# Forty-eight projections a layer placed between the steps of an attention, and its head norm taken with tokens on partitions

## The reference

```python
h = rmsnorm(x, norm_g)
aq, ak, av, az, bqk, bv, bi, bf, bo, bz, ga, gb = split(h @ w_in)      # 1024 -> 10256
# branch a: 8 heads, two score maps of 64 each, values of 128
q, k = rope(rmsnorm(aq)), rope(rmsnorm(ak))
a = softmax(causal(q1 k1')) - lam * softmax(causal(q2 k2'))
oa = rmsnorm(a @ av, attn_norm_g) * (1 - lam_init) * silu(az)
# branch b: mLSTM of 8 heads, in its quadratic form
mq, mk = split(silu(causal_conv(bqk, conv_w, conv_b)))                 # 4 taps
hb = (mq mk' * exp(gates)) @ bv / max(|row sum|, exp(-m))
hb = sigmoid(bo) * rmsnorm(hb, mlstm_norm_g) * silu(bz)
u = sigmoid(ga) * (oa @ w_out_a) + sigmoid(gb) * (hb @ w_out_b)
x = x + u @ w_o
```

## Time and profile before

| | |
|---|---|
| median of three runs | 2130.93 us |
| profiled execution, span | 2131.4 us |
| PE busy | 2042.5 us (96%) |
| DVE, ACT, POOL busy | 1151.3, 909.2, 291.2 us |
| the two attentions of the second block | 110.3 and 110.8 us, to the last scores' transposes |

### The profile page before, as it was taken

How to read it: one execution, slowest core, us unless ns; L and a number is a source line. 1 busy time by engine, 2 the same in 40 slices (tenths; PEclk the granted TensorE clock), 3 DMA queues, 4 the chain that set the end, 5 groups by cost and what they waited for, 6 DMA issues and landing times.

```text
span 2131.4 us, 28672 instructions
## 1 busy us (share of the span) xinstructions
PE 2042.5 (96%) x11112; PEld 1557.0 (73%) x11112; DVE 1151.3 (54%) x2057; ACT 909.2 (43%) x1685; POOL 291.2 (14%) x354
## 2 busy tenths in 40 slices
PE   7999999899999998999999899999999899999998
PEld 2443334378888885546899899995599899975798
DVE  3327442287777532462555575665545677555544
ACT  2235331151423324452555565544453565545442
POOL 1015000000000000230000042202213052002303
PEclk9999999989999999999999999995599999975799
DMA  8320232234554431201454443540044334520141
GB/s 295 110 79 33 87 119 79 79 119 163 192 186 170 158 95 47 79 1 41 157 190 167 159 153 135 197 159 1 1 158 170 137 130 153 214 80 1 58 180 60
DMA packets 139874, 255.27 MB, mean 120 GB/s; under 512 B 14926, under 2 KB 21724, under 8 KB 139612
## 3 DMA queue, kind: packets, MB, share of 16 engines
q1 hardware_dynamic: 138742, 251.16, 33.5%
q0 software_dynamic: 704, 2.10, 0.3%
q10 hardware_dynamic: 294, 0.18, 0.0%
HBM read 252.38 MB, written 1.05 MB: 119 GB/s over the span
## 4 chain that ended last, share of the span: by engine, by line
PE 89%; DVE 5%; ACT 3%; POOL 2%; issue 1%; DMA 1%; POOLq 0%; SPq 0%; DVEq 0%; ACTq 0%
PE ps L1033 15%; PE ps L1035 15%; PE ps L1034 15%; PE ps L1042 9%; PE ps L928 5%; PE ps L984 4%; PE ps L1173 3%; PE ps L1147 3%; PE ps L1312 3%; PE ps L1159 2%; PE ps L1316 1%; PE ps L1320 1%; PE ps L945 1%; PE ps L1243 1%; PE ps L1244 1%; PE ps L1245 1%
## 5 line engine op out<-in xcount | busy, mean ns | idle before, releaser
L1830 DVE TENSOR_TENSOR big_r<-ring,big_r 128x1024 fp32r<-128x1024 f32 x232 | 286.6, 1237 | 292.2 <-ACT big_r L1421 292.1
L1421 ACT ACTIVATE big_r<-ring 128x1024 fp32r<-128x1024 f32 x232 | 245.5, 1060 | 452.1 <-PE ps L1035 434.8
L1034 PE MATMUL ps<-big_r 128*128 128x256 f32 (+1 forms) x1184 | 392.3, 331 | 0.0
L1033 PE MATMUL ps<-hT_r,big_r 128*128 128x256 f32 (+1 forms) x1056 | 335.5, 318 | 14.3 <-DVE big_r L1839 10.8
L1035 PE MATMUL ps<-hT_r,big_r 128*128 128x256 f32 (+1 forms) x1056 | 329.3, 312 | 0.0
L1034 PEld LDWEIGHTS ps<-big_r 128*128 128x128 f32 x1184 | 227.5, 192 | 19.4
L1033 PE MATMUL ps<-big_r 128*128 128x256 f32 (+1 forms) x688 | 223.9, 325 | 6.0 <-POOL xT_r L892 4.6
L1033 PEld LDWEIGHTS ps<-hT_r,big_r 128*128 128x128 f32 x1056 | 204.4, 194 | 31.9 <-issue 15.9
L1035 PE MATMUL ps<-big_r 128*128 128x256 f32 (+1 forms) x688 | 222.6, 324 | 0.0
L1042 PE MATMUL ps<-hT,ring 128*128 128x512 f32 (+2 forms) x576 | 206.3, 517 | 11.2 <-ACT hT L1442 9.4
L1035 PEld LDWEIGHTS ps<-hT_r,big_r 128*128 128x128 f32 x1056 | 204.6, 194 | 10.5
(11 more groups left out here) (252 smaller groups left out, 3952.3 us busy)
## 6 DMA issues: line engine op xcount, KB each, us to landing
ring<-in_w_in SPq DMA_DIRECT2D x42, 2048.0 KB, 7.8
ring<-in_w_mlp SPq DMA_DIRECT2D x32, 2048.0 KB, 8.3
ring<-in_w_mod SPq DMA_DIRECT2D x24, 2048.0 KB, 7.9
ring<-in_w_out SPq DMA_DIRECT2D x4, 2048.0 KB, 7.7
ring<-in_w_out_a SPq DMA_DIRECT2D x4, 2048.0 KB, 7.6
ring<-in_w_out_b SPq DMA_DIRECT2D x4, 2048.0 KB, 7.7
ring<-in_w_o SPq DMA_DIRECT2D x4, 2048.0 KB, 7.7
ring<-in_w_in SPq DMA_DIRECT2D x12, 256.0 KB, 4.8
```

The source lines that it names most:

```text
L1033: mm(b[:, 0:T], w_hi[:, k, :], hi(k), start=(k == 0), stop=False)
L1034: mm(b[:, 0:T], w_hi[:, k, :], lo(k), start=False, stop=False)
L1421: act_fn(hi, raw, ACT.Copy).then_inc(hi_ready, 1)
L1830: V.tensor_tensor(lo, raw, hi.bitcast(F32), ALU.subtract).then_inc(lo_ready, 1)
```

## The change

The steps of the attention number 37 (`STEPS`). The products of az, bqk, bo, bz, ga and gb, 48 a layer (`MID`), are spread over them: `mid_of(step)` gives each step one product (`first`), and eleven of the steps a second (`others`). With bv ahead of bif, all that is left before the attention is aq, ak, av, bv and bif; behind it outa, outb and wo. In a step PE takes: scores, the first product, the transposes of unit step - 3, then in odd steps the product with the values and in even steps (from step 6) the transposes of the normed head, then the second product, if any. ACT and DVE follow the same order, with the granule work and evictions of `projected` at the product's place. Steps 6, 10, 16, 20, 26, 30 are the even ones with a second product from step 6 on, steps 13, 23, 33 the odd ones.

The product with the values is turned: `pT` is the stationary side, so tokens lie on partitions. ACT squares with `accum_out` (two instructions of 128 x 128), which gives a mean square per token. DVE takes the inverse root in `root_of_mean`: a first guess from the bits of the number, three Newton steps, all on [128, 2], and two passes that scale the product; PE transposes the result back; DVE applies gain and gate in one pass (`gate`), and POOL is left with the split. The division by the softmax sums and by the mLSTM denominator moves into these scales: `stat` has 8 places, not 4.

The three weight buffers lie elsewhere, one chain of them serves the whole layer, and the table of ScalarE functions is loaded once for the attention. The numbers of the diff's other lines (buffer places, semaphores) are left out.

```diff
+MID_SLOTS = [("az", 0), ("bqk", 0), ("az", 1), ("bqk", 1), ("bo", 0), ("bz", 0), ("bo", 1), ("bz", 1),
+             ("ga", 0), ("ga", 1), ("gb", 0), ("gb", 1)]
+MID = [(name, 4 * n + m) for name, n in MID_SLOTS for m in range(4)]
+UNITS = 4 * NH2
+STEPS = UNITS + 5
+def mid_of(step):
+    lo, hi = (min(len(MID), -(-len(MID) * s // STEPS)) for s in (step, step + 1))
+    return MID[lo:hi][:1], MID[lo:hi][1:]
...
@@ TensorE
-                features_product("az", h_hi_at, h_lo_at)
-                features_product("bz", h_hi_at, h_lo_at)
...
+                for step in range(STEPS):
+                    first, others = mid_of(step)
...
+                    for name, c in first:
+                        split_product(gran_of[(tag, name, c)], h_hi_at, h_lo_at, SEQ)
...
-                        mm(b[:, 0:SEQ], vt[:, 0, h * P:(h + 1) * P], pT[:, p % 2, 0, :], start=True, stop=False)
-                        fill(mm(b[:, P:SEQ], vt[:, 1, h * P:(h + 1) * P], pT[:, p % 2, 1, P:SEQ], start=False,
+                        mm(b[:, 0:P], pT[:, p % 2, 0, 0:P], vt[:, 0, h * P:(h + 1) * P], start=True, stop=True)
+                        mm(b[:, P:SEQ], pT[:, p % 2, 0, P:SEQ], vt[:, 0, h * P:(h + 1) * P], start=True, stop=False)
+                        fill(mm(b[:, P:SEQ], pT[:, p % 2, 1, P:SEQ], vt[:, 1, h * P:(h + 1) * P], start=False,
                                 stop=True), (tag, "o", p))
                     if 0 <= p < 2 * NH2 and odd:
-                        squares((tag, "oms", p), cc("ones"), P, SEQ, 1)
+                        b = start_bank((tag, "oT", p))
+                        pe.wait_ge(on_ready, 2 * NH2 * l + p + 1)
+                        for i in range(2):
+                            last = tr(b[:, i * P:(i + 1) * P], on[:, p % 2, i, :], IDENT)
+                        fill(last, (tag, "oT", p))
+                    for name, c in others:
+                        split_product(gran_of[(tag, name, c)], h_hi_at, h_lo_at, SEQ)
@@ ScalarE
+                        await_bank(act, (tag, "o", p))
+                        for i in range(2):
+                            r = 8 * ((2 * p + i) % 8) + 6
+                            act_fn(osq[:, i, :], bank((tag, "o", p))[:, i * P:(i + 1) * P], ACT.Square,
+                                   scale=stat[:, r:r + 1], accum_out=rn[:, 0, i:i + 1]).then_inc(ms_ready, 1)
@@ VectorE
+                def root_of_mean(p):
...
+                    dve.wait_ge(ms_ready, 4 * NH2 * l + 2 * p + 2)
+                    link(V.tensor_scalar(x, ms, 1.0 / P, EPS, ALU.mult, ALU.add))
+                    link(V.tensor_scalar(y.bitcast(I32), x.bitcast(I32), -0.5, ROOT_SEED, ALU.mult, ALU.add))
+                    link(V.tensor_scalar(x, x, -0.5, None, ALU.mult))
+                    for _ in range(3):
+                        link(V.tensor_tensor(ms, y, y, ALU.mult))
+                        link(V.tensor_tensor(ms, ms, x, ALU.mult))
+                        link(V.scalar_tensor_tensor(y, ms, 1.5, y, ALU.add, ALU.mult))
+                    link(V.tensor_tensor(y, y, r, ALU.mult))
...
+                        last = V.tensor_scalar(on[:, p % 2, i, :], bank(key)[:, i * P:(i + 1) * P], y[:, i:i + 1], None,
+                                               ALU.mult)
...
-                            link(V.tensor_scalar(w, w, st[:, 7:8], small[:, 2:3], ALU.mult, ALU.mult))
-                            V.scalar_tensor_tensor(a, a, st[:, 6:7], w, ALU.mult, ALU.add).then_inc(p_ready, 1)
+                            link(V.scalar_tensor_tensor(st[:, 5:6], st[:, 4:5], st[:, 7:8], small[:, 2:3], ALU.mult, ALU.mult))
+                            V.scalar_tensor_tensor(a, w, st[:, 5:6], a, ALU.mult, ALU.add).then_inc(p_ready, 1)
...
+                    if 0 <= p < 2 * NH2 and odd:
+                        root_of_mean(p)
+                    for name, c in first:
+                        projected(name, c)
+                    if 0 <= p < 2 * NH2 and odd:
+                        gate(p)
+                    for name, c in others:
+                        projected(name, c)
```

More of the change, by code:

```diff
@@ L259, in plan_banks @@
             take((tag, "t", u), 4)
+        take((tag, "gT"), 5)
         for p in range(2 * NH2):
-            take((tag, "o", p), 5 + p % 2)
-            take((tag, "oms", p), 7)
-        for name in ("ga", "gb", "outa", "outb", "wo"):
+            take((tag, "o", p), 5)
+            take((tag, "oT", p), 5)
+        for j, (name, c) in enumerate(MID):
+            take((tag, name, c), 6 + j % 2)
+        for name in AFTER:
             for c in range(8):
@@ L277, in mlp_slots, with tanh_order @@
     return order
-BEFORE = ("aq", "ak", "av", "bqk", "bo", "bif", "bv", "az", "bz")
-AFTER = ("ga", "gb", "outa", "outb", "wo")
+BEFORE = ("aq", "ak", "av", "bv", "bif")
+MID_SLOTS = [("az", 0), ("bqk", 0), ("az", 1), ("bqk", 1), ("bo", 0), ("bz", 0), ("bo", 1), ("bz", 1),
+             ("ga", 0), ("ga", 1), ("gb", 0), ("gb", 1)]
+MID = [(name, 4 * n + m) for name, n in MID_SLOTS for m in range(4)]
+AFTER = ("outa", "outb", "wo")
+UNITS = 4 * NH2
[3 more added lines that the diff above has]
+    return MID[lo:hi][:1], MID[lo:hi][1:]
+def tanh_order():
+    order, late = [], None
+    for name, c in MID:
+        if name in ("az", "bz"):
+            order.append((name, c))
+        if late is not None:
+            order.append(("bqk", late))
+        late = c if name == "bqk" else None
+    return order
 MLP_BUFS, B_BUFS = 2, 3
@@ L299, in granules_b @@
     b = ("b", l)
[L300 removed]
+    before = []
     for name in BEFORE:
[L302 to L309 removed]
         if name == "bif":
@@ L693, in program @@
                     order += [((tag, n, "ms"), 1, (tag, n, 0)) for n, _, _ in units_b()]
-                    order += [((tag, "oms", p), 1, (tag, "o", p)) for p in range(2 * NH2)]
                 for key, chunks, applied in order:
@@ L1647, in _ @@
+                    if late[0] is not None:
+                        act.wait_ge(z_ready, 8 * l + late[0] + 1)
+                        tanh_of(("bqk", late[0]), mqkT[:, late[0], :], 1.0)
+                    late[0] = c if name == "bqk" else None
+                for step in range(STEPS):
+                    first, others = mid_of(step)
+                    if step < UNITS:
+                        u = step
                         p, i = divmod(u, 2)
                         h, keys = p % NH2, (i + 1) * P
-                        st = stat[:, 8 * (u % 4):8 * (u % 4) + 8]
+                        st = stat[:, 8 * (u % 8):8 * (u % 8) + 8]
@@ L2091, in _ @@
+                for step in range(STEPS):
+                    first, others = mid_of(step)
+                    if step < UNITS and step // 2 < NH2:
+                        u = step
                         i = u % 2
                         keys = (i + 1) * P
-                        st = stat[:, 8 * (u % 4):8 * (u % 4) + 8]
+                        st = stat[:, 8 * (u % 8):8 * (u % 8) + 8]
                         await_bank(dve, (tag, "s", u, 0))
```

430 lines of the change are left out of this document (202 added, 228 removed).

## The result

The changed kernel takes 2213.57 us, the median of four runs (2212.08 to 2226.83); the kernel before took 2131.39 beside it (2130.35 to 2132.56). The ratio is 1.039, with a 95% interval of 1.036 to 1.042: 82 us slower. The forecast was 2161, its range 2105 to 2205. The direction held, and so did the chain from one head to the next; how often the clock falls, and the front of the stretch, did not.

What follows compares the result with a forecast made beforehand. PE at half clock bounded the attention; interleaved, PE would wait for a chain through ACT and DVE. 2131.4 + 16 (chain, 262 us a layer against 254) + 14 (clock falls) = 2161 us, range 2105 to 2205.

Steps and rivals of the forecast that it cites:

- The direction: Whole kernel: the change makes it slower, 2161 us against 2131.4; chance of slower 0.70.
- What bounds the kernel before, and what PE gains: Second block's attentions: PE at half clock bounds; interleaving, if PE never waited, takes 207 us a layer, 47 less than 254.
- The chain of a pair: From one head's root to the next on DVE: 12.95 us + e (eviction) in branch a, 12.3 + e in b; PE's work 10.0.
- step 2: ACT's rounding waits for the exponential, so DVE is past the rest 3.6 us after the product, not 2.6; branch b 3.1.
- The clock: PE in the interleaved attention: some waits lose the full clock, 2.0 us a fall, 7 us a layer, 14 in all.
- half of the seven gaps: Share taken to lose the clock among a layer's seven gaps between products longer than 5.1 us; 7 us a layer.
- The front of the stretch: Ahead of the first head: eight products, six scores, transposes and the chain's first part, 42.3 us a layer.
- step 3: Projection's eviction on DVE: 0.4 us for az, nothing for bo, ga, gb, 0.9 for bz, 2.1 for a convolution.
- a rival at 2211: PE in the attention: the clock falls in every pair, 2131.4 + 16 + 64 = 2211 us; chance 0.10.
- my reading of one row: Kernel before, layer 0's scores: light work of some 5 us after the last product loses the clock once.
- Contention with POOL: POOL's silus and splits beside DVE's granule work: at worst 0.5 us a pair, 8 a layer; taken as 0.

Runs made afterwards that it cites:

- a cut of 37 us in the waits: One Newton step of the root in place of three, against the kernel as changed: 2145.5 us, ratio 1.007 to the kernel before.
- the kernel ordered by the chain: Against the changed kernel: transposes, scores and values' product ahead of each step's product, root and gate ahead of granule work, two Newton steps; 2077.7 us, ratio 0.972.

## Why the prediction was wrong

- *What bounds the kernel before, and what PE gains.* Right. PE at half clock set the attention; once the chain no longer stands in the way, the interleaving gives 54 us of the 94 counted (2131.4 to 2077.7; 63 against the 2140.5 that the kernel before took beside it).
- *The chain of a pair.* Right, and nearly to the number: 3.5 us for step 2 where 3.6 stood, 2.56 for the root where 2.5 stood, waits of 59 us a layer in the range of 45 to 60. Two sizes in it had no row behind them, and came out as taken: 0.03 between linked instructions on 128 x 2 is 0.035 (0.195 from one to the next, 0.19 taken), and the 0.2 until PE sees the signal is 0.2 (1478.95 to 1479.15).
- *The clock: the step that failed.* I took "half of the seven gaps" longer than 5.1 us, 7 us a layer, because layer 0's scores had lost the clock some 5 us after a product. That measured a stretch of light work; the gaps of the changed kernel hold idle time of PE as well, and the clock went down behind 12 of the 16 waits: in all seven of those gaps and in five that I had not counted. The size of one fall was right (2.2 us in the nine that the added matmuls took away, 2.0 taken), the number was not: 3.5 a layer taken, 12 measured, with one more in the front. The added matmuls gave 41 us back and left three of the twelve in each layer; with these and the one in the front all falls of the stretch come to some 26 us a layer, 52 for both, where I had 14 (an estimate from 20.1, 4.6 and 1.4 us). That is 38 of the 54 us by which the two stretches are longer than counted. A further fall behind POOL's split, in outa's first product, stands outside the stretch.
- *The front of the stretch.* The other failure. It took 51.1 us (1336.21 to 1387.32) where 42.3 stood. Of the 8.8 us, 1.4 are the fall already counted. The rest, 7.4 a layer and 15 for both, is PE's wait of 2.7 us behind ACT's gates and table load, a path on which the prediction had put nothing, and the ring of the four convolutions. In step 3 a convolution was priced at 2.1 us, at the two heads it precedes; it took 2.7, and each of the four stood on the chain. Together 38 + 15 = 53 of the 54.
- *The rule on the clock.* "TensorE: Matmul & The Clock Gate" in the Trainium skill, section "HAM oscillation — how this bites in real kernels", says that waits between bursts of matmuls lose the clock again and again. The prediction cited it for a rival at 2211 and gave that 0.10. The runs agree with the rule more than with my reading of one row: falls in 12 of 16 gaps, and none behind a head whose wait filler work had cut to 1.4 us or less. But three waits of 2.35 to 2.40 us in each layer kept the clock, and in the kernel ordered by the chain one product in layer 0 is slow behind a wait of 0.79 us (the one that starts at 1397.55), so the runs bear out neither "at each wait" nor a length below which it is safe. The rival's total came within 3 us of the measured time partly by luck: its sum has 64 us of falls, where about 52 were found in the stretch; the rest was the front.
- *Contention with POOL* was taken as 0. It costs 3.2 us a layer in the front, a part of the 7.4 above; between the heads it stays open.

## What to carry to other kernels

When work of another stage is interleaved into a chain, write down for each engine what its list holds ahead of the instruction that the bounding engine waits for: here the same instructions in another order were worth 132 us (2213.6 to 2081.8). Take idle time of TensorE twice, once as it is and once as the clock that it costs behind it: a cut of 37 us in the waits gave 68. And count the start of an interleaved stretch by itself, with what now stands ahead of it on each engine. And look at runs of equal, heavy items (four convolutions in a row) apart from the mean pair, since they can close a ring between two engines that are idle for 40% (DVE) and 64% (ACT) of the stretch.

## What was not expected of the hardware

- A DVE instruction on 128 x 2 that takes 0.16 us took 0.57 beside POOL's silu, and a first tap 0.82 in place of 0.41:

```profile
1384.77 0.16 DVE L2129 TENSOR_TENSOR rn<-rn 128x2 f32<-128x2 f32 x1
1384.97 0.57 DVE L2130 TENSOR_TENSOR rn<-rn 128x2 f32<-128x2 f32 x1
```

- Useless matmuls paid: 18 of them in each wait, 2.4 us, made the kernel 41 us faster.
- Equal waits did not cost the clock alike: in each layer three of 2.35 to 2.40 us with a product right behind the transposes kept it, and one of 2.38 or 2.40 us with scores behind the transposes lost it.
